# A transformer block with experts on one core: ring rooms given to the experts one by one, the first modulation sum moved into attention, router weights held stationary

## The chip, the core and the metric

The kernel runs on one core of a Trainium2 chip. Its engines are TensorE (PE), VectorE (DVE), ScalarE (ACT), GpSimd (POOL) and SyncE (SP), which here issues nearly all weight loads. The metric is the time of one execution on the device in microseconds, lower is better. The time before is 2291.39 us, the median of 3 runs (2287.88 to 2292.07).

## The reference, cut to what matters

512 tokens of width 1024, all in float32. A first block mixes tokens by attention and a gated linear recurrence, then sends tokens to 16 experts; a second block follows (convolution, pooling and a dense feed-forward part) that the change does not touch.

```python
mod = (silu(c) @ ada_w + ada_b)                      # ada_w is (1024, 6144)
shift1, scale1, gate1, shift2, scale2, gate2 = split(mod, 6)
h = rms_norm(x, norm_mix_w) * (1 + scale1) + shift1
# token_mixer: projections by w_in, attention o_att, recurrence o_hg, then
merged = sigmoid(g0) * (o_att @ w_branch_att) + sigmoid(g1) * (o_hg @ w_branch_hg)
x = x + gate1 * (merged @ w_out)
h = rms_norm(x, norm_ffn_w) * (1 + scale2) + shift2
# expert_choice_ffn
affinity = softmax(h @ w_router)                     # (512, 16)
top_w, top_idx = top_k(affinity.T, 64)               # each expert takes 64 tokens
hid = silu(h[top_idx] @ w_gate[e]) * (h[top_idx] @ w_up[e])    # 64 x 2048
x = x + gate2 * scatter_add(top_w * (hid @ w_down[e]))
```

## The kernel before

Everything is written engine by engine, with semaphores between engines; no scheduler moves anything. The order of work on an engine is the order of its code, partly woven from generators by `weave`, which takes one step of each in turn.

**The ring.** All weights arrive in pieces of 1 MB (128 partitions x 2048 floats) in rooms of SBUF called slots. There are 15: slots 0 to 5 are the ring proper, slots 6 to 14 lie in the work area and become free only when the token mixer's tensors there are dead. `ring_plan` writes down, for each piece, its slot; SP goes through that list in order (L385 to L402), waits for the last reader of the piece that was in the slot (`last_reader`), and issues the load. As SP works in order, a piece whose slot is not free holds back all behind it. An expert has 24 pieces, `eg` and `eu` (a gate and an up piece for each of 8 blocks k of the input width) and 8 of `ed` (down); 16 experts have 384. The first 15 go to rooms named by `cycle`; from then on a piece waits for the one 15 places ahead of it to be read.

**The modulation (ada).** `ada_w` comes as 24 pieces, 8 for each third of `mod`. `ada_step` on DVE (L1449) multiplies a piece by a column of silu(c) and adds it to an accumulator of 128 x 2048. Two sums over the partitions follow on PE: `ada_cols` (L423, L425) gives 8 columns by matmuls that move one column each, and a bias by one-row matmuls; `ada_row` (L698, L699) gives a row of 512 repeated on all partitions, by a matmul with a stationary block of ones and one with a one-row bias. Pieces 8 to 15 give gate1 and shift2, pieces 16 to 23 give scale2 and gate2.

**The merge loop**, `for d in range(8)` at L702: eight blocks of 128 output channels. For d of 4 and more PE first computes the two gate projections (`c0`, `c1`), then for all d the two branch projections (`cb`, first half into bank b0+2, second into b0+3). DVE multiplies and adds them (L1644, L1646, L1649, semaphores mg_a, mg_b, mg_m) and then takes ada steps: 1 after each of d = 0 to 3, 3 after each of d = 4 to 7. After d = 5 PE runs `ada_row` and `ada_cols` on the first sum, after d = 7 `ada_cols` and `ada_row` on the second.

**From w_out to the experts.** `out_proj` (L758) makes 8 units u of w_out, DVE adds each to x (L1673, L1675), and then x is normed, transposed by PE (`turn`, L437), scaled by DVE and ACT by turns into H2T, and `logits(k)` (L799) multiplies block k of H2T by 16 columns of the router's weights, two blocks behind the transposes. DVE takes the softmax and then finds 64 tokens for each of 16 experts by eight rounds of max and match_replace (L1701, L1702); L817 turns the mask, L822 counts positions. `gather` (L837) then picks the tokens, and the experts start (L879 gate and up, L915 down).

Attention and the second half of the recurrence run before the merge loop in one weave, on each engine:

```python
            weave(fill, lv, fill, att, fill, att, fill)
```

Here `lv` is a level of the recurrence (DVE: L1554 to L1572), `att` a step of attention (DVE: L1600 to L1607), `fill` the gate projections of PE (L622).

Of the kernel before, what the change touches and what calls it, by code (L numbers as in the profile page):

```python
# [10 lines left out]
ALU = mybir.AluOpType  # L11
# [58 lines left out]
MG, ACC2 = QQ, TTA  # L70
X = QT
# [29 lines left out]
def ring_plan():  # L101
# [7 lines left out]
    more = [("bg", h, br) for h in range(2) for br in range(2)]  # L109
    ada = 8  # L110
    for half in range(4):
        if half >= 2:
            more += [("c0", half), ("c1", half)]
        more.append(("cb", half))
        n = 2 if half < 2 else 6
        more += [("ada", ada + i) for i in range(n)]
        ada += n
    slots += [(4, 5, 0, 1, 2)[i % 5] for i in range(len(more))]
    keys += more + [("wo", n) for n in range(4)]
    slots += [3, 1, 2, 4]  # L120
# [5 lines left out]
    cycle = (11, 12, 13, 14, 5, 0, 3, 1, 2, 4, 7, 8, 9, 10, 6)  # L126
# [60 lines left out]
def build(nc, t, out):  # L187
    with ExitStack() as ctx:
# [194 lines left out]
        def _(e):  # L383
            for key, (slot, _, before) in plan.items():
# [21 lines left out]
        def _(e):  # L406
# [284 lines left out]
            def ada_row(half, dst_n):  # L691
                for i in range(2):
                    n, bk = half * 1024 + 512 * i, 2 + i

                    e.wait_ge(s["mg_a" if i == 0 else "mg_b"], 5 if half == 0 else 7)
                    if half == 1:
                        e.wait_ge(s["ar_a"], i + 1)
                    e.matmul(bank(bk), ones, at(ACC2 + n, 512), start=True, stop=False)  # L698
                    e.matmul(bank(bk), one_row, rows(0, 1, ADAB + n, 512), start=False, stop=True).then_inc(s["ar_pe"], 1)  # L699


            for d in range(8):  # L702
# [20 lines left out]
                if j == 0:  # L723
                    e.wait_ge(*got[kb])

# [6 lines left out]
                else:  # L732
                    e.wait_ge(s["mg_a"], d - 1)
                    if d == 6:
                        e.wait_ge(s["ar_a"], 1)
# [3 lines left out]
                elif d >= 2:  # L739
                    e.wait_ge(s["mg_b"], d - 1)  # L740
                    if d == 6:
                        e.wait_ge(s["ar_a"], 2)
                    if d == 7:
                        e.wait_ge(s["ad_d"], 1)
# [1248 lines left out]
```

## Time and profile before

| | |
|---|---|
| median of 3 runs | 2291.39 us |
| the profiled execution, its own time | 2292.04 us |
| its span in the profile | 2290.2 us |
| PE busy | 2031.2 us (89%), 8478 instructions |
| DVE busy | 606.4 us (26%) |
| ACT busy | 412.6 us (18%) |
| DMA | 513.37 MB, 224 GB/s over the span |
| the chain that ended last | PE 71%, DMA 18%, DVE 5%, ACT 4% |

A float32 matmul is two records of a MATMUL and of a weight load each, so counts in the rows below are twice those of the code. The clock column PEclk gives the granted TensorE clock as a share: 1.00 is the level of 2.4 GHz, 0.50 that of 1.2 GHz. A stretch in the windows view lists busy time and instructions of PE, PE's weight loads, DVE, ACT and POOL, then PEclk, the share of DMA and GB/s. In the order rows further down, which show the program and no time, a matmul is one row.

### The profile page before, as it was taken

Reading aid. Unit: us, or ns where it says so; the run is one execution under the profiler, and the core shown is the slowest. Engines: PE = TensorE matmul, PEld = TensorE weight load, DVE = VectorE, ACT = ScalarE, POOL = GpSimd, SP = SyncE. Lnnn points to the kernel's source line nnn. Section 1 sums busy time; section 2 is a strip of 40 time slices with the busy share of each in tenths; the row PEclk is TensorE's granted clock in tenths of the full one; section 3 lists DMA queues with packets and bytes.
Section 4 is the critical chain, followed back from the end, with each engine's and each line's share of the span. In section 5 each row is a group of like instructions: output and inputs, shape, how many; then the busy total and the mean of one; then the engine's idle time right before and its main releaser. Section 6 shows DMA issues by size and latency. Waiting matters only on the chain.

```text
span 2290.2 us, 19692 instructions
## 1 busy us (share of the span) xinstructions
PE 2031.2 (89%) x8478; PEld 1145.7 (50%) x8478; DVE 606.4 (26%) x867; ACT 412.6 (18%) x621; POOL 32.8 (1%) x42
## 2 busy tenths in 40 slices
PE   3986999999897998888888889888879998999997
PEld 2543465544486343434343434233334487888785
DVE  4152335332323001010101111100127714222233
ACT  2123545510011000000000000000020213222222
POOL 0000000000000000000000000000030000000000
PEclk9998999997795999999999999999989998999998
DMA  8210111134632999999999999999962123322210
GB/s 327 74 37 19 37 37 56 37 111 165 249 130 91 416 416 416 416 416 416 416 416 416 416 416 416 416 416 417 417 219 74 37 68 93 97 92 93 91 37 37
DMA packets 143787, 513.37 MB, mean 224 GB/s; under 512 B 7891, under 2 KB 70355, under 8 KB 107731
## 3 DMA queue, kind: packets, MB, share of 16 engines
q1 hardware_dynamic: 141632, 503.35, 56.2%
q10 hardware_dynamic: 2070, 8.78, 0.9%
q8 instruction: 67, 1.10, 0.2%
q14 instruction: 18, 0.15, 0.0%
HBM read 510.00 MB, written 2.10 MB: 224 GB/s over the span
## 4 chain that ended last, share of the span: by engine, by line
PE 71%; DMA 18%; DVE 5%; ACT 4%; issue 1%; SPq 1%; POOL 0%; ACTq 0%; DVEq 0%; POOLq 0%
PE ps L412 14%; DMA work<-in_w_exp_up 11%; PE ps L915 11%; PE ps L879 6%; PE ps L417 6%; DMA ring<-in_w_exp_up 6%; PE ps L1058 5%; PE ps L1017 4%; PE ps L1019 4%; PE ps L1018 4%; PE ps L837 3%; PE ps L622 2%; DMA ring<-in_ada_w 2%; PE ps L567 1%; PE ps L860 1%
## 5 line engine op out<-in xcount | busy, mean ns | idle before, releaser
L879 PE MATMUL ps<-work 128*64 128x512 f32 x1232 | 312.9, 595 | 43.2 <-DMA work<-in_w_exp_up 43.2
L412 PE MATMUL ps<-work,ring 128*128 128x512 f32 x784 | 344.6, 598 | 0.8 <-DVE work L1588 0.8
L412 PEld LDWEIGHTS ps<-work,ring 128*128 128x128 f32 x784 | 149.0, 192 | 187.8 <-issue 186.1
L879 PE MATMUL ps<-ring,work 128*64 128x512 f32 x816 | 217.4, 595 | 24.3 <-DMA ring<-in_w_exp_up 24.3
L879 PEld LDWEIGHTS ps<-work 128*64 128x64 f32 x1232 | 107.3, 137 | 220.7 <-issue 138.8
L1750 DVE TENSOR_TENSOR work<-work,ps 64x512 f32<-64x512 f32 x64 | 42.0, 691 | 507.9 <-ACT work L1320 507.3
L1320 ACT ACTIVATE work<-ps 64x512 f32<-64x512 f32 x64 | 32.6, 584 | 758.4 <-PE ps L879 758.4
L915 PE MATMUL ps<-work 128*64 128x512 f32 x600 | 143.1, 634 | 5.2 <-issue 4.7
L879 PEld LDWEIGHTS ps<-ring,work 128*64 128x64 f32 x816 | 74.6, 137 | 140.6 <-issue 92.5
L417 PE MATMUL ps<-ring,work 128*128 128x256 f32 x640 | 142.8, 386 | 0.9 <-ACT work L1350 0.9
L1017 PE MATMUL ps<-xh,wh 128*128 128x512 f32 x352 | 137.8, 391 | 1.0 <-issue 1.0
L1018 PE MATMUL ps<-xl,wh 128*128 128x512 f32 x352 | 137.6, 391 | 0.0
L1019 PE MATMUL ps<-xh,wl 128*128 128x512 f32 x352 | 137.4, 390 | 0.0
L417 PEld LDWEIGHTS ps<-ring,work 128*128 128x128 f32 x640 | 123.8, 194 | 22.4 <-issue 5.2
L1854 DVE TENSOR_TENSOR wl<-ring,wh 128x2048 fp32r<-128x2048 f32 x32 | 73.4, 2292 | 186.3 <-ACT wh L1389 186.3
L915 PE MATMUL ps<-ring,work 128*64 128x512 f32 x424 | 100.3, 628 | 3.1 <-issue 3.1
L1058 PE MATMUL ps<-wh,xh 128*128 128x512 f32 x352 | 96.4, 396 | 5.6 <-issue 5.6
L915 PEld LDWEIGHTS ps<-work 128*64 128x64 f32 x600 | 53.0, 145 | 86.8 <-issue 86.8
L1762 DVE TENSOR_TENSOR work<-ps,stay 64x512 f32<-64x512 f32 x32 | 22.0, 688 | 276.1 <-PE ps L915 275.6
L1389 ACT ACTIVATE wh<-ring 128x2048 fp32r<-128x2048 f32 x33 | 63.1, 1913 | 176.1 <-PE ps L1019 93.9
L1058 PEld LDWEIGHTS ps<-wh,xh 128*128 128x128 f32 x352 | 67.3, 192 | 20.1 <-issue 6.0
L860 PE MATMUL ps<-work 128*128 128x512 f32 x128 | 66.4, 630 | 9.7 <-DVE work L1741 8.1
(229 smaller groups left out, 1928.5 us busy)
## 6 DMA issues: line engine op xcount, KB each, us to landing
work<-in_w_exp_gate SPq DMA_DIRECT2D x77, 1024.0 KB, 23.0
work<-in_w_exp_up SPq DMA_DIRECT2D x77, 1024.0 KB, 23.2
work<-in_w_exp_down SPq DMA_DIRECT2D x75, 1024.0 KB, 21.0
ring<-in_w_exp_down SPq DMA_DIRECT2D x53, 1024.0 KB, 20.9
ring<-in_w_exp_gate SPq DMA_DIRECT2D x51, 1024.0 KB, 22.7
ring<-in_w_exp_up SPq DMA_DIRECT2D x51, 1024.0 KB, 23.2
ring<-in_w_in SPq DMA_DIRECT2D x27, 1024.0 KB, 6.9
ring<-in_ada_w SPq DMA_DIRECT2D x24, 1024.0 KB, 5.6
```

The lines of the kernel that those rows point to most:

```text
L412: i = e.matmul(bank(bk), piece(key)[:, off + k, 128 * j:128 * j + 128], rhs(k), start=(k == 0), stop=(k == nk - 1))
L417: i = e.matmul(bank(bk, n, o), lhs(k, tc), piece(key)[:, k, c0:c0 + n], start=(k == 0), stop=(k == 7))
L837: i = e.matmul(bank(5 + k // 4, 128, 128 * (k % 4)), at(XS2 + 1024 * c + 128 * k, 128), at(OH + 128 * c, 128), start=(c == 0), stop=(c == 3))
L860: e.matmul(bank(6 + dh), at(OHWT + 128 * tc, 128), at(YE + 512 * dh, 512), start=True, stop=True).then_inc(s["x_cb"], 1)
L879: i = e.matmul(PS[64 * gu:64 * gu + 64, fb, :], at(XET + 128 * k + 64 * z, 64), flat(key)[:, 512 * fb:512 * fb + 512], start=(k == 0), sto ...
L915: i = e.matmul(PS[64 * dh:64 * dh + 64, 4, :], at(HIDT + 64 * (2 * n + k), 64), piece(key, 2)[:, k, 512 * dh:512 * dh + 512], start=(n + k ...
L1017: e.matmul(bank(bk), WH[i][:, o:o + 128], XH[:, x], start=(k == 0), stop=False)
L1018: e.matmul(bank(bk), WH[i][:, o:o + 128], XL[:, x], start=False, stop=False)
L1019: p = e.matmul(bank(bk), WL[i][:, o:o + 128], XH[:, x], start=False, stop=(k == KD - 1))
L1058: p = e.matmul(bank(2 * tc + dh), l[:, o], w[i][:, 1024 * k + 512 * dh:1024 * k + 512 * dh + 512], start=(f == 0 and q == 0), stop=(f == F ...
L1389: e.activation(WH[i][:, :], flat(("ff", f)), ACT.Copy).then_inc(s["fs_h"], 1)
L1854: e.tensor_tensor(WL[i][:, :], flat(("ff", f)), WH[i][:, :].bitcast(F32), ALU.subtract).then_inc(s["fs_l"], 1)
```

## The change

1. **Rooms one by one.** The order in which the first 15 expert pieces take rooms is new, and each room of the work area has a wait of its own instead of one for nearly all of them. Most of them are now asked for before or early in w_out.
2. **First modulation sum during attention.** Pieces 8 to 15 go into an accumulator of their own, ACC1, in the room of GATE1 and GATE2, one step for each round of the weave. Their two sums on PE move from behind d = 5 into d = 6. The second sum's steps follow 1, 1, 1, 1, 2, 2 times after d = 0 to 5 and no longer after d = 6 and 7; its sums on PE stand behind units 1 and 2 of w_out. DVE's scale2 comes after unit 1.
3. **Stationary router weights.** `logits(k)` is one matmul that holds 16 columns of the router stationary and moves 512 tokens, in place of four that hold 128 tokens and move 16 columns. The logits then lie with experts on partitions; a copy by DVE and four transposes (`by_token`) bring them back. The counting of positions takes 4 matmuls of 64, 48, 32 and 16 columns in place of 10 of 16.
4. x is loaded before the merge loop in place of after it, and DVE's scratch in w_out moves from PT to YE.

```diff
+ACC1 = GATE1
-    slots += [(4, 5, 0, 1, 2)[i % 5] for i in range(len(more))]
-    slots += [3, 1, 2, 4]
+    bg = [("bg", h, br) for h in range(2) for br in range(2)]
+    ada = lambda i: [(("ada", 8 + 2 * i), 4), (("ada", 9 + 2 * i), 5)]
+    more = [(bg[0], 0)] + ada(0) + [(bg[1], 1), (bg[2], 2)] + ada(1) + [(bg[3], 0)] + ada(2)
+    rest = [("cb", 0), ("cb", 1), ("c0", 2), ("c1", 2), ("cb", 2), ("c0", 3), ("c1", 3), ("cb", 3)]
+    for i, key in enumerate(rest):
+        more += [(key, (1, 2, 0)[i % 3])] + (ada(3 + i) if i < 5 else [])
+    more += [(("wo", n), (3, 4, 5, 0)[n]) for n in range(4)]
-    cycle = (11, 12, 13, 14, 5, 0, 3, 1, 2, 4, 7, 8, 9, 10, 6)
+    cycle = (8, 11, 12, 13, 14, 10, 9, 1, 2, 7, 3, 4, 5, 0, 6)
...
-                if key[0] in ("eg", "eu") and before is None and slot >= 11:
-                    e.wait_ge(s["mg_pb"], 8)
-                if key[0] in ("eg", "eu") and before is None and 6 <= slot <= 10:
-                    e.wait_ge(s["wo_pe"], 8)
-                    e.wait_ge(s["wo_x"], 8)
-                    e.wait_ge(s["ar_pe"], 4)
-                    if slot == 6:
+                if key[0] in ("eg", "eu") and before is None:
+                    if slot == 8:
+                        e.wait_ge(s["mg_m"], 1)
+                    elif slot >= 11:
+                        e.wait_ge(s["mg_pb"], 8)
+                    elif slot >= 9:
+                        e.wait_ge(s["mg_m"], 8)
+                    elif slot == 7:
+                        e.wait_ge(s["ac_pe"], 3)
+                        e.wait_ge(s["ar_pe"], 4)
+                    elif slot == 6:
+                        e.wait_ge(s["wo_pe"], 8)
                         e.wait_ge(s["rt_pe"], 1)
...
+                if d == 6:
+                    e.wait_ge(s["d_ada"], 16)
+                    e.wait_ge(s["l_ab"], 32)
+                    e.wait_ge(s["mg_a"], 6)
+                    ada_row(ACC1, 0, 6)
+                    e.wait_ge(s["mg_b"], 6)
+                    ada_row(ACC1, 512, 7)
...
+                if d == 6:
+                    e.wait_ge(s["ar_a"], 1)
+                    ada_cols(ACC1, 1, 6, 0, True).then_inc(s["ac_pe"], 1)
+
+            def second_gate(u):
+                if u == 1:
+                    e.wait_ge(s["d_ada"], 24)
+                    e.wait_ge(s["l_ab"], 48)
+                    e.wait_ge(s["mg_b"], 8)
+                    ada_cols(ACC2, 0, 7, 0, True).then_inc(s["ac_pe"], 1)
+                    e.wait_ge(s["mg_a"], 8)
+                    ada_row(ACC2, 1024, 6)
+                elif u == 2:
+                    e.wait_ge(s["ad_d"], 2)
+                    ada_row(ACC2, 1536, 7)
...
-                for tc in range(TC):
...
-                    p = e.matmul(bank(4 + tc, 16), at(H2T + 512 * k + 128 * tc, 128), at(O_VEC + VEC["wr"][0] + 16 * k, 16),
-                                 start=(k == 0), stop=(k == KD - 1))
+                return e.matmul(PS[0:16, 4, :], at(O_VEC + VEC["wr"][0] + 16 * k, 16), at(H2T + 512 * k, 512), start=(k == 0), stop=(k == KD - 1))
...
-            for tc in range(TC):
-                for c in range(tc + 1):
-                    p = e.matmul(bank(4, 16, 16 * tc), tri if c == tc else ones, at(mskT + 16 * c, 16), start=(c == 0), stop=(c == tc))
+            for back in range(TC):
+                p = e.matmul(bank(4, 64 - 16 * back, 16 * back), tri if back == 0 else ones, at(mskT, 64 - 16 * back), start=(back == 0), stop=(back == 3))
...
+            def ada_first():
+                for i in range(8, 16):
+                    ada_step(i, ACC1)
+                    yield
-            weave(fill, lv, fill, att, fill, att, fill)
+            weave(fill, lv, fill, att, fill, att, fill, ada_first())
...
-                for _ in range(1 if d < 4 else 3):
+                for _ in range(1 if d < 4 else 2 if d < 6 else 0):
...
+            e.wait_ge(*rooted(2, 3))
+            e.tensor_copy(rows(0, 16, WKT, 512), PS[0:16, 4, :]).then_inc(s["rt_d"], 1)
```

On PE, from the merge loop's last blocks to w_out, before (L412 is a dense block of the merge loop, 8 rows to a projection of eight blocks k; L698, L699 are `ada_row`, L423, L425 `ada_cols`, L417 w_out):

```order
L412 MATMUL ps<-work,ring 128x512 x80
L698 MATMUL ps<-work,stay 128x512
L699 MATMUL ps<-work,stay 128x512
L423 MATMUL ps<-stay,work 128x1
L425 MATMUL ps<-stay,work 128x1
...
L412 MATMUL ps<-work,ring 128x512 x48
L423 MATMUL ps<-stay,work 128x1
L425 MATMUL ps<-stay,work 128x1
...
L698 MATMUL ps<-work,stay 128x512
L699 MATMUL ps<-work,stay 128x512
L417 MATMUL ps<-ring,work 128x256 x128
```

The same place of the change, where these lines are L416, L696, L697, L427, L429 and L421:

```order
L416 MATMUL ps<-work,ring 128x512 x96
L696 MATMUL ps<-stay 128x512
L697 MATMUL ps<-work,stay 128x512
...
L416 MATMUL ps<-work,ring 128x512 x8
L427 MATMUL ps<-stay 128x1
L429 MATMUL ps<-stay,work 128x1
...
L416 MATMUL ps<-work,ring 128x512 x24
L421 MATMUL ps<-ring,work 128x256 x32
...
L421 MATMUL ps<-ring,work 128x256 x16
...
L421 MATMUL ps<-ring,work 128x256 x80
```

The first `ada_row` now has 16 more dense matmuls ahead of it, 8 dense ones stand between it and `ada_cols`, and d = 7 runs straight into w_out, whose units 0 and 1 (x32) and 2 (x16) come ahead of the second sum's parts.

On DVE, one round of the attention weave: before, the last share of attention (L1607) is followed at once by the next level of the recurrence (L1554).

```order
L1600 TENSOR_REDUCE stay<-ps 128x1
L1601 TENSOR_SCALAR stay<-stay 128x1
L1606 RECIPROCAL stay<-stay 128x1
L1607 TENSOR_SCALAR work<-work,stay 128x512
L1554 TENSOR_TENSOR work<-work 128x2x128x4
```

In the change (L1616 is the share, L1563 the level) an ada step stands between them, once in each of eight rounds.

```order
L1609 TENSOR_REDUCE stay<-ps 128x1
L1610 TENSOR_SCALAR stay<-stay 128x1
L1615 RECIPROCAL stay<-stay 128x1
L1616 TENSOR_SCALAR work<-work,stay 128x512
L1465 SCALAR_TENSOR_TENSOR stay<-ring,stay 128x2048
L1563 TENSOR_TENSOR work<-work 128x2x128x4
```

On PE, the router before: transposes (L437), four logits matmuls a block (L799), then the turns of the affinities and of the mask, and the ten of the count.

```order
L437 MATMUL ps<-stay,work 128x128 x4
L799 MATMUL ps<-stay,work 128x16 x12
L813 MATMUL ps<-stay 16x128 x4
L817 MATMUL ps<-stay,work 128x16 x4
L822 MATMUL ps<-stay 128x16 x10
L837 MATMUL ps<-work 128x128 x32
```

And in the change: one matmul a block (L804), one more set of turns (the first L816), and four for the count (L831).

```order
L441 MATMUL ps<-stay,work 128x128 x4
L804 MATMUL ps<-work,stay 16x512 x3
L816 MATMUL ps<-stay,work 128x16 x4
L824 MATMUL ps<-stay 16x128 x4
L816 MATMUL ps<-stay,work 128x16 x4
L831 MATMUL ps<-stay 128x64
L831 MATMUL ps<-stay 128x48
L831 MATMUL ps<-stay 128x32
L831 MATMUL ps<-stay 128x16
L846 MATMUL ps<-work 128x128 x32
```

## Rows read from the trace of the kernel before

**Rows 1.** Windows: the last router stretch, the first experts, the other experts.

```profile
709.00:741.30 32.30, 18.44 (x106) 15.81 (x108) 14.36 (x33) 2.79 (x5) 0.00 (x0) 0.63 0.02 9
741.30:841.00 99.70, 95.30 (x486) 41.79 (x482) 10.52 (x18) 9.03 (x21) 0.00 (x0) 0.98 1.01 409
841.00:1683.00 842.00, 742.79 (x3422) 306.98 (x3418) 109.95 (x176) 60.95 (x143) 0.00 (x0) 0.98 1.01 413
```

**Rows 2.** Timeline of SP's issues, 607 to 745 us: start, us, what.

```profile
612.78 0.43 SPq L402 DMA_DIRECT2D ring<-in_w_exp_up  x1
...
705.61 0.33 SPq L402 DMA_DIRECT2D work<-in_w_exp_gate  x1
...
741.34 0.33 SPq L402 DMA_DIRECT2D work<-in_w_exp_up  x1
```

**Rows 3.** The chain that ended last, 532 to 681 us: start, us, what.

```profile
532.70 0.70 DVE work L1646
...
534.18 2.27 DVE work L1456
...
552.79 44.47 PE ps L412 x96
...
597.64 6.99 DMA ring<-in_ada_w
...
604.72 2.36 DVE work L1456
...
623.42 57.33 PE ps L417 x256
```

**Rows 4.** Windows: ada_row, ada_cols, then dense work at the higher clock.

```profile
536.00:544.50 8.50, 8.00 (x8) 2.00 (x8) 0.44 (x1) 0.60 (x1) 0.00 (x0) 0.50 1.04 378
544.50:552.70 8.20, 8.20 (x33) 7.96 (x32) 0.00 (x0) 0.60 (x1) 0.00 (x0) 0.50 0.51 162
560.00:565.00 5.00, 5.00 (x13) 2.20 (x12) 0.00 (x0) 0.60 (x1) 0.00 (x0) 1.00 0.18 77
630.00:680.00 50.00, 50.00 (x234) 44.01 (x233) 11.43 (x18) 4.06 (x7) 0.00 (x0) 1.00 0.30 112
```

**Rows 5.** The chain near the start: ada_cols, transposes, dense matmuls, all at clock 1.00.

```profile
35.51 6.99 PE ps L423 x32
42.49 5.76 PE ps L437 x32
48.26 41.20 PE ps L412 x96
```

**Rows 6.** Timeline of DVE: a round of the attention weave, and an ada step.

```profile
375.03 0.49 DVE L1607 TENSOR_SCALAR work<-work,stay 128x512 f32<-128x512 f32 x1
378.53 1.23 DVE L1554 TENSOR_TENSOR work<-work 128x1024 f32<-128x1024 f32 x1 [3.01 <-PE ps L567]
...
479.16 2.35 DVE L1456 SCALAR_TENSOR_TENSOR work<-ring,stay,work 128x2048 f32<-128x2048 f32 x1
```

**Rows 7.** The chain in the logits: one block's transposes, then its matmuls.

```profile
689.81 0.93 PE ps L437 x4
690.74 1.52 PE ps L799 x8
```

**Rows 8.** Windows: the logits as a whole.

```profile
690.00:705.00 15.00, 15.00 (x75) 15.00 (x73) 1.62 (x2) 3.61 (x4) 0.00 (x0) 0.50 0.37 153
```

**Rows 9.** The chain in the routing: a copy of 16x512, mask turns, position count.

```profile
708.15 0.69 DVE work L1698
...
721.27 0.62 PE ps L817 x4
...
722.19 4.46 PE ps L822 x20
```

**Rows 10.** Windows: transposes alone ahead of the second block, then what follows.

```profile
1702.50:1705.50 3.00, 3.00 (x16) 3.00 (x15) 1.13 (x2) 1.37 (x2) 3.00 (x6) 0.50 0.00 0
1706.00:1709.00 3.00, 3.00 (x14) 1.77 (x13) 0.96 (x3) 1.33 (x2) 3.00 (x6) 1.00 0.02 5
```

More of the change, by code:

```diff
@@ L108, in ring_plan @@
     slots = [i % 6 for i in range(len(keys))]
[L109 to L117, printed above, removed]
-    slots += [(4, 5, 0, 1, 2)[i % 5] for i in range(len(more))]
-    keys += more + [("wo", n) for n in range(4)]
-    slots += [3, 1, 2, 4]
+    bg = [("bg", h, br) for h in range(2) for br in range(2)]
[5 more added lines that the diff above has]
+    more += [(("wo", n), (3, 4, 5, 0)[n]) for n in range(4)]
+    keys += [key for key, _ in more]
+    slots += [slot for _, slot in more]
     ex = []
@@ L689, in _, with ada_row @@
             weave(fill, lv, fill, att, fill, att, fill)
[L691 to L699, printed above, removed]
+            def ada_row(acc, n, bk):
+                e.matmul(bank(bk), ones, at(acc + n, 512), start=True, stop=False)
+                e.matmul(bank(bk), one_row, rows(0, 1, ADAB + n, 512), start=False, stop=True).then_inc(s["ar_pe"], 1)
             for d in range(8):
@@ L769, in out_proj @@
                         p.then_inc(done, 1)
+                        behind(4 * h + n)
             def wo_free(u):
@@ L1649, in _ @@
                 e.tensor_tensor(at(MG + 512 * d, 512), at(s0, 512), at(s1, 512), ALU.add).then_inc(s["mg_m"], 1)
-                for _ in range(1 if d < 4 else 3):
-                    if ada == 16:
-                        e.wait_ge(s["ac_pe"], 2)
-                        e.tensor_copy(at(sh2, 8), bank(7, 8)).then_inc(s["ad_d"], 1)
+                for _ in range(1 if d < 4 else 2 if d < 6 else 0):
                     ada_step(ada, ACC2)
                     ada += 1
-            e.wait_ge(s["ac_pe"], 3)
-            e.scalar_tensor_tensor(out=at(sc2, 8), in0=bank(7, 8), scalar=1.0, in1=vec("nfw"),
-                                   op0=ALU.add, op1=ALU.mult).then_inc(s["ad_d"], 1)
+                if d == 6:
+                    e.wait_ge(s["ac_pe"], 2)
+                    e.tensor_copy(at(sh2, 8), bank(6, 8)).then_inc(s["ad_d"], 1)
             e.wait_ge(s["l_x"], 32)
@@ L1675, in _ @@
                     e.tensor_tensor(xa, xa, ta, ALU.add).then_inc(s["wo_x"], 1)
+                    if u == 1:
+                        e.wait_ge(s["ac_pe"], 3)
+                        e.scalar_tensor_tensor(out=at(sc2, 8), in0=bank(7, 8), scalar=1.0, in1=vec("nfw"),
+                                               op0=ALU.add, op1=ALU.mult).then_inc(s["ad_d"], 1)
                 def r2_ready(c):
@@ L1695, in _ @@
             e.tensor_tensor(r3(aff), r3(lg), r16(rst + 8), ALU.mult).then_inc(s["rt_d"], 1)
-            e.wait_ge(s["rt_pe"], 2)
-            e.wait_ge(*rooted(2, 3))
-            own(e.tensor_copy(rows(0, 16, AFFT, 512), PS[0:16, 5, :]))
+            e.wait_ge(s["rt_pe"], 3)
+            own(e.tensor_copy(rows(0, 16, AFFT, 512), PS[0:16, 4, :]))
             for r in range(CAP // 8):
```

84 lines of the change are left out of this document (35 added, 49 removed).

## Prediction

> **What bounds the kernel now.** I read the windows by stage first, then SP's issues, then the chain of waits. From 741.3 to 1683 us DMA is busy all the time and moves 409 to 413 GB/s [rows 1]: the experts are bound by their weights. When that stretch begins is decided on PE. SP issues the last of the first 15 expert pieces at 705.61, has no free room left, and issues the 16th only at 741.34, when PE has read the first piece [rows 2]; in between DMA is idle (9 GB/s from 709 to 741.3, [rows 1]). From there the remaining 369 pieces of 1 MB follow at a fixed rate (1683 - 741.3 = 942 us, 2.55 us a piece), and behind them comes a second block that nothing here touches. So a microsecond gained ahead of 741 is gained at the end, one for one, and the date at which the first 15 pieces land is worth nothing as long as they are there. The sum is therefore one about the chain from the merge loop to the first gather.
>
> In that chain [rows 3] two waits stand out. PE has finished d = 5 at 532.67; then come DVE's L1646 (0.70), L1649 (as long) and an ada step (2.27), and `ada_row` starts at 536.50, a stall of 3.8 us. After d = 7, at 597.3, PE waits for an ada piece (DMA, to 604.63) and its step (2.36), 9.9 us. The windows add a third cost: after each stall the granted clock is 0.50, through `ada_row` and `ada_cols`, and back at 1.00 only some us into dense work [rows 4].
>
> **Rooms one by one: nothing.** The edit moves issues of expert pieces earlier, into idle DMA time. What hides it is the wait for room number 16, above. The last room, slot 6, is still tied to `rt_pe` 1, and 15 pieces are read in the old order of positions afterwards. x comes earlier too; it delayed only DVE. Both 0.
>
> **Ada steps in attention: nothing, under a thin cover.** A step is 2.35 us of DVE. In each round DVE is idle for 3.01 us at just the place where it goes, between L1607 and L1554 [rows 6]; that round stands for eight, the others read 3.0 to 3.9 or more, and the first step is a short one. So it ends about 0.6 us before the level's matmul that DVE waits for. The pieces: two rooms (4, 5) go round between eight steps 12 us apart, and a piece needs 7 us (6.99, [rows 3]). Without that cover, each round would pay up to 2.4 us, 19 us in all.
>
> **The chain from 532.67 to 680.75.** It takes 148.1 us now. Prices at clock 1.00: a dense record of 512 columns 0.43 (41.20 / 96, [rows 5]), one of w_out 0.214 (50 / 234, [rows 4]); `ada_cols`, 32 records, 7.0 at 1.00 [rows 5] and 8.2 at 0.50 [rows 4]; `ada_row`, 8 records for two rows, 8.1 at 0.50 (from 536.5 to 544.6, [rows 4]). At 1.00 no row shows it: at least 8 x 0.43 = 3.4, at most the 8.1; I take 4.1, half and nearest the dense record, as the same columns move. What a restart of the clock costs: 44.47 - 96 x 0.43 = 3.2 in d = 6 and 7, 57.33 - 256 x 0.214 = 2.6 in w_out [rows 3].
>
> New: the gate projections of d = 6, 32 x 0.43 = 13.8; `ada_row` behind them without a stall (its own steps are over since attention, and DVE's work after d = 5, the merge and two steps, is 6.2 us beside 13.8 us of PE), at 1.00, 4.1; the branch projections 6.9; `ada_cols` 7.6 (it starts at 1.00 and ends, I assume, at 0.50); d = 7 20.6 + 2.9 for the restart; then a new wait, since w_out's unit 0 stands straight behind d = 7 and needs the merged block: L1646 and L1649, 1.5; units 0 and 1, 13.7; `ada_cols` 7.6; first half of the second `ada_row` at 0.50, 4.0; unit 2, 6.9 + 2.6; second half at 1.00, 2.1; units 3 to 7, 34.2. The sum is 128.5, **19.6 less**. Queued behind the wait on DVE for `ac_pe` 3 (after unit 1) are only the sums of units 2 and later, which PE reaches 14 us later.
>
> **Routing.** The copy of 16x512 (0.69) and the turns back (0.62) are new on the path, 1.4 with their hand-overs. The count has 8 records in place of 20: 4.46 x 12/20 = 2.7 less [rows 9]. Together **1.3 less**.
>
> **Logits.** Now a block takes 4 transposes (0.93) and 8 records (1.52), 2.45, so 19.6 for eight [rows 7], all at clock 0.50 [rows 8]. New: 0.93 and 2 records that move 512 columns. At 0.50 such a record costs between 0.86 (twice 0.43) and 1.01 (8.1 / 8 in `ada_row`); at 0.95 a block is 2.83, eight are 22.6, **3.0 more**. The question is whether the clock stays. The old loop moves 16 columns at a time and kept 0.50 for 15 us of unbroken work [rows 8]. The new loop is made of transposes and 512-column matmuls. Transposes alone are shown to bring the clock back: in 1702.5 to 1705.5 PE does 16 of them and nothing else at 0.50, and then stands at 1.00 [rows 10]. For dense matmuls of 512 and 256 columns it came back too [rows 4]. It did not come back in `ada_row`, half of whose matmuls have one row. So I expect it back some 5.5 us into the loop, as the restarts above cost 2.6 to 3.2 us, half of their length. Then at 1.00 a block costs 4 x 0.18 (5.76 / 32, [rows 5]) + 0.86 = 1.6: 5.5 + 9.2 = 14.7, **4.9 less**.
>
> A page speaks against this step. The Trainium skill, "TensorE: Matmul & The Clock Gate", Part 4, says that a transpose does not count as busy time for the clock gate. This case's trace does not agree ([rows 10], 0.50, then 1.00 with transposes alone before). By the page's rule the transposes would not help and the clock would likely stay at 0.50, so that the sum would be 3.0 more and not 4.9 less, case (a) below.
>
> **Sum.** 19.6 + 1.3 + 4.9 = 25.8 from the profiled execution's own 2292.04 gives 2266.2; the median before is 0.65 lower, so 2265.6. I say 2266.
>
> **The rivals.**
> (a) The clock stays at 0.50 in the logits, since a matmul with 16 stationary columns may not act as a full one: 19.6 + 1.3 - 3.0 = 17.9 less, 2273.5. For it: no row here has 16 stationary columns and many moved ones.
> (b) The clock does not fall in `ada_cols` when it enters at 1.00. The only `ada_cols` at 1.00 is [rows 5], and the clock stayed there, but PE had had nothing to do in the 35 us ahead of it, and it had stayed through that as well. Then the restarts (2.9 + 2.6), twice 0.6 of `ada_cols` and 2 of the half row fall away: 7 to 9 more, 2258.
> (c) The cover in attention is too thin, or DVE is late for w_out: part is given back. A third of the saving lost is 8 us; with half a dozen rounds late by 2 us, 12. 2276 to 2288. The cover of 3.01 against 2.35 speaks against it.
> (d) The change does not do what it says for the total: the expert stream is not released by PE but ends at its own date, so that PE only waits longer at the experts. Then 2291, no change. The idle DMA from 709 to 741.3 [rows 1] speaks against it.
> (e) Slower: DVE works in order, so when an ada step's piece has not landed in a round, attention and the recurrence both stand. Two rooms serve the eight steps, and SP takes the branch gates' pieces in the same list ahead of some of them, so that a piece can hang on a room that PE frees a round later. It decides from 25.8 / 8 = 3.2 us a round beyond the gap on; a full round late (12 us) in three rounds would be 36 less 26, 2301. By the list the pieces are asked for 20 us or more ahead of their step, which speaks against it.
>
> **How the numbers follow.** The main case (back in the logits, down in `ada_cols`) has 0.48, and by itself runs from 2262 to 2270 (ada_row between 3.4 and 8.1, restarts between 2.6 and 3.2, record between 0.86 and 1.01). (a) 0.23, (b) 0.14, (c) 0.09, (d) 0.03, (e) 0.03. The range of 8 in 10 takes the main case, (a) whole and most of (b): 2257 to 2277. A measurement of this kernel can tell 0.2%, 4.6 us, from no change. Faster by more: the first three and all of (c), 0.94; within it (d), 0.03; slower (e), 0.03.
>
> **What the profile of the changed kernel would show.** PE without a gap from d = 0 to the end of d = 7, then 1.5 us idle before w_out. Clock 1.00 in the first `ada_row`, and four records of it per 2 us. The 16th expert piece issued at about 715 to 717, the DMA then at 410 GB/s for 942 us as before. In attention, DVE's ada steps between L1616 and L1563 with some 0.6 us of idle left, and PE with no new wait there. In the logits blocks of 2.8 us first and of 1.6 us later, or of 2.8 throughout in case (a). The prediction is wrong if the stretch from the 16th piece to the end of the experts is not 942 us, if PE waits in attention, or if the clock drops in places where PE is now meant to run through.

## The result and the profile after

The changed kernel takes 2252.91 us (median of 4 runs, 2251.59 to 2256.67), the kernel before beside it 2291.14 us: a ratio of 0.9838, 95% interval 0.9821 to 0.9855. That is 38.2 us less, where I had forecast 25 and a range that ended at 2257. Two repeats of the unedited change, told below, gave 2254.30 and 2258.05 us; the median of all 12 runs of it is 2255.3. The profiled execution took 2251.97 us with a span of 2250.2, 40.0 less than the span before.

The chain that ended last, from the merge loop to the end of w_out, in the changed kernel (start, us, what):

```profile
466.55 79.23 PE ps L416 x184
545.79 0.86 PE ps L696 x2
546.65 1.05 PE ps L697 x2
...
549.80 7.06 PE ps L416 x16
...
556.98 0.31 PE ps L429 x2
...
561.63 22.51 PE ps L416 x48
...
584.16 0.70 DVE work L1661
...
585.79 14.05 PE ps L421 x64
...
602.79 0.52 PE ps L427 x2
...
605.87 2.01 PE ps L696 x2
...
609.88 8.57 PE ps L421 x32
618.45 0.86 PE ps L696 x2
...
620.35 34.74 PE ps L421 x160
```

Against [rows 3] both stalls are gone: dense work runs unbroken from 466.55 to 545.79, through the place where PE used to stop at 532.67, and between d = 7 and w_out only the merge (1.6 us) is left. The first `ada_row` takes 4.0 us for its two rows (0.86 to 1.05 a pair of records) in place of 8.1.

The same chain through the router:

```profile
660.46 2.10 PE ps L441 x9
662.55 1.70 PE ps L804 x2
664.25 0.59 PE ps L441 x4
664.85 0.96 PE ps L804 x2
...
671.05 2.69 PE ps L804 x6
...
673.76 0.69 DVE work L1706
...
674.50 0.43 PE ps L816 x4
...
691.20 1.90 PE ps L831 x8
...
694.36 9.20 PE ps L846 x64
703.56 27.67 PE ps L888 x128
```

The first logits matmul still runs at the lower clock (1.70 us a pair), all later ones at the higher (0.96, then 0.90), and four transposes fall from 0.93 to 0.59 [rows 7]. The windows say the same (columns as in [rows 1]):

```profile
549.80:556.80 7.00, 7.00 (x19) 3.17 (x18) 0.69 (x1) 0.60 (x1) 0.00 (x0) 1.00 0.00 0
556.87:561.60 4.73, 4.73 (x33) 4.49 (x32) 1.38 (x2) 0.00 (x0) 0.00 (x0) 1.00 0.01 3
561.63:564.00 2.37, 2.37 (x3) 1.09 (x4) 0.17 (x1) 0.00 (x0) 0.00 (x0) 0.50 0.01 3
...
664.30:673.70 9.40, 9.40 (x34) 2.93 (x34) 1.62 (x2) 3.61 (x4) 0.00 (x0) 1.00 0.01 2
```

`ada_cols` (556.87 to 561.6) begins at 1.00, the clock falls at its end, and d = 7 starts at 0.50. In the router the clock is back at 1.00.

SP's issues of the 15th and 16th expert pieces, which answer to [rows 2]:

```profile
673.82 0.33 SPq L406 DMA_DIRECT2D work<-in_w_exp_gate  x1
707.17 0.33 SPq L406 DMA_DIRECT2D work<-in_w_exp_up  x1
```

The 16th goes out at 707.17 in place of 741.34, 34.2 us earlier. From the merge loop's start to the first gate and up matmul it is now 237.0 us (466.55 to 703.56), before 270.6 (467.16 to 737.73). I use that distance below, as it leaves out what shifts the start of the loop from one execution to the next (465.7 to 468.0).

| stretch | before | after | less | forecast |
|---|---|---|---|---|
| up to the merge loop | 467.2 | 466.6 | 0.6 | 0 |
| merge loop and w_out | 213.6 | 188.6 | 25.0 | 19.6 |
| norm (to the first transposes) | 5.4 | 5.4 | 0 | 0 |
| logits | 19.4 | 13.3 | 6.1 | 4.9 |
| softmax, choice, count | 22.4 | 20.6 | 1.8 | 1.3 |
| first gather | 9.8 | 9.2 | 0.6 | 0 |
| first gate matmul to the end | 1552.5 | 1546.6 | 5.9 | 0 |

So two things have to be explained: 7.7 us more than forecast ahead of the experts, and 5.9 from the first gate matmul on, where nothing was changed.

### The profile page after: what moved, and what is told of

It is laid out like the page before. It is cut to its first block, busy times and chain, and to the rows that moved or that the text cites. A ratio compares the mean times of both kernels' runs of the same rounds, so it can differ in the third digit from the quotient of the medians.

```text
span 2250.2 us, 19571 instructions
## 1 busy us (share of the span) xinstructions
PE 2005.9 (89%) x8422; PEld 1117.0 (50%) x8422; DVE 606.8 (27%) x868; ACT 412.6 (18%) x621; POOL 32.7 (1%) x42
## 4 chain that ended last, share of the span: by engine, by line
PE 71%; DMA 18%; DVE 5%; ACT 4%; issue 1%; SPq 0%; POOL 0%; ACTq 0%; DVEq 0%; POOLq 0%
PE ps L416 15%; DMA work<-in_w_exp_up 13%; PE ps L924 11%; PE ps L888 7%; PE ps L421 6%; PE ps L1067 5%; DMA ring<-in_w_exp_up 4%; PE ps L1026 4%; PE ps L1028 4%; PE ps L1027 4%; PE ps L846 3%; PE ps L626 3%; PE ps L571 1%; DMA ring<-in_ada_w 1%; PE ps L869 1%
## 5 line engine op out<-in xcount | busy, mean ns | idle before, releaser
L888 PE MATMUL ps<-work 128*64 128x512 f32 x1256 | 351.6, 595 | 40.3 <-DMA work<-in_w_exp_up 40.3
L416 PE MATMUL ps<-work,ring 128*128 128x512 f32 x784 | 344.6, 598 | 0.8 <-DVE work L1597 0.8
L888 PE MATMUL ps<-ring,work 128*64 128x512 f32 x792 | 242.6, 595 | 23.7 <-DMA ring<-in_w_exp_up 23.7
L416 PEld LDWEIGHTS ps<-work,ring 128*128 128x128 f32 x784 | 149.0, 192 | 187.9 <-issue 186.3
L888 PEld LDWEIGHTS ps<-work 128*64 128x64 f32 x1256 | 116.0, 137 | 230.3 <-issue 154.0
L888 PEld LDWEIGHTS ps<-ring,work 128*64 128x64 f32 x792 | 80.5, 137 | 128.1 <-issue 82.3
L421 PE MATMUL ps<-ring,work 128*128 128x256 f32 x640 | 141.3, 383 | 2.5 <-DVE work L1664 1.7
L924 PE MATMUL ps<-work 128*64 128x512 f32 x600 | 140.0, 618 | 3.7 <-issue 3.1
L421 PEld LDWEIGHTS ps<-ring,work 128*128 128x128 f32 x640 | 122.2, 192 | 24.9 <-issue 8.4
L924 PE MATMUL ps<-ring,work 128*64 128x512 f32 x424 | 108.0, 658 | 4.7 <-issue 4.7
L924 PEld LDWEIGHTS ps<-work 128*64 128x64 f32 x600 | 52.2, 143 | 84.5 <-issue 84.5
## 6 DMA issues: line engine op xcount, KB each, us to landing
ring<-in_w_exp_up SPq DMA_DIRECT2D x51, 1024.0 KB, 22.4
```

The costliest lines, as they stand in the source:

```text
L416: i = e.matmul(bank(bk), piece(key)[:, off + k, 128 * j:128 * j + 128], rhs(k), start=(k == 0), stop=(k == nk - 1))
L421: i = e.matmul(bank(bk, n, o), lhs(k, tc), piece(key)[:, k, c0:c0 + n], start=(k == 0), stop=(k == 7))
L888: i = e.matmul(PS[64 * gu:64 * gu + 64, fb, :], at(XET + 128 * k + 64 * z, 64), flat(key)[:, 512 * fb:512 * fb + 512], start=(k == 0), sto ...
L924: i = e.matmul(PS[64 * dh:64 * dh + 64, 4, :], at(HIDT + 64 * (2 * n + k), 64), piece(key, 2)[:, k, 512 * dh:512 * dh + 512], start=(n + k ...
```

## The experiments

In the runs named e1 to e12 the kernel before took 2291.6 to 2292.7 us beside them, in the last four 2291.47.

**e1, the router alone.** The kernel before with part 3 of the change and nothing else:

```diff
-                    p = e.matmul(bank(4 + tc, 16), at(H2T + 512 * k + 128 * tc, 128), at(O_VEC + VEC["wr"][0] + 16 * k, 16),
-                                 start=(k == 0), stop=(k == KD - 1))
+                return e.matmul(PS[0:16, 4, :], at(O_VEC + VEC["wr"][0] + 16 * k, 16), at(H2T + 512 * k, 512), start=(k == 0), stop=(k == KD - 1))
...
+            by_token()
...
+            for back in range(TC):
+                p = e.matmul(bank(4, 64 - 16 * back, 16 * back), tri if back == 0 else ones, at(mskT, 64 - 16 * back), start=(back == 0), stop=(back == 3))
```

> The kernel before with the third part alone (stationary router weights, logits turned back, four matmuls for the count). My theory: the first gather comes 7.5 to 8.5 us earlier (logits 13.3 us in place of 19.4, from the copy to the count 20.6 in place of 22.4) and the total follows one for one: 2283 us. Rival: the parts lean on each other, because the clock enters the logits in another state in the old surroundings; then the clock stays at 0.50 and the total is 2291 to 2294.

It took 2283.64 us against 2292.70, ratio 0.9959 (0.9947 to 0.9972), 9.1 us less; the distance was 263.7 us (466.59 to 730.26), 6.9 less than before and a little under the 7.5 I gave. The part works by itself. What is missing lies in the logits: they took 14.4 us, as the clock came back 6.4 us into them (first group of four transposes at 0.59 us at 691.93, first transpose at 685.50), where in the change it came back after 3.8 us and they took 13.3.

**e2, the router undone.** The changed kernel with the old router.

```diff
-                return e.matmul(PS[0:16, 4, :], at(O_VEC + VEC["wr"][0] + 16 * k, 16), at(H2T + 512 * k, 512), start=(k == 0), stop=(k == KD - 1))
+                for tc in range(TC):
...
+                    p = e.matmul(bank(4 + tc, 16), at(H2T + 512 * k + 128 * tc, 128), at(O_VEC + VEC["wr"][0] + 16 * k, 16),
+                                 start=(k == 0), stop=(k == KD - 1))
```

> The changed kernel with the old router. My theory: rooms and modulation sums are worth 25 us of chain and 2 to 6 us of clock in later stages, so 2260 to 2263 us. Rival (the parts do not add up): the two parts alone sum to clearly less or more than the 38 us of both.

2265.04 us, ratio 0.9877 (0.9863 to 0.9890); distance 244.4 us (467.82 to 712.21), 26.2 less. 26.2 and 6.9 are 33.1, both together gave 33.6: the parts add up. The total was 2 us above what I expected, since that had the 2 to 6 us of later stages in it.

**e3, late rooms.** The changed kernel with the waits for rooms of before:

```diff
-                    if slot == 8:
-                        e.wait_ge(s["mg_m"], 1)
...
+                if key[0] in ("eg", "eu") and before is None and 6 <= slot <= 10:
+                    e.wait_ge(s["wo_pe"], 8)
+                    e.wait_ge(s["wo_x"], 8)
+                    e.wait_ge(s["ar_pe"], 4)
-    cycle = (8, 11, 12, 13, 14, 10, 9, 1, 2, 7, 3, 4, 5, 0, 6)
+    cycle = (11, 12, 13, 14, 1, 2, 3, 4, 5, 0, 7, 8, 9, 10, 6)
```

> The changed kernel with the old waits for the rooms of the work area, so that only 4 expert pieces are asked for before the first w_out units end and 10 come after unit 6 or later. My theory: all 15 are in SBUF before the first gather ends, the 16th is asked for at the same time, and the total stays within 1 us of 2253. Rival (the rooms matter): the experts' first pieces are late, or DMA runs behind from the start, and the total rises by the amount of weights not loaded by then, up to 10 pieces or 25 us.

The distance was 237.1 us (468.04 to 705.14) against 237.0: the early rooms are worth nothing, as they only fill time in which DMA would otherwise load later and still in time. The total was 2258.64 us (2253.89 to 2259.24). That is not within 1 us of 2253, and at first it looked like a cost of 5 us; the last four runs below show that it is the other length of the last stretch, here 1552.1 us.

**e4, the second sums ahead of w_out.**

```diff
+            second_gate(1)
+            second_gate(2)
-            out_proj("wo", lambda k, tc: at(MG + 512 * k + 128 * tc, 128), s["wo_pe"], wo_free, lambda: e.wait_ge(s["mg_m"], 8), second_gate)
+            out_proj("wo", lambda k, tc: at(MG + 512 * k + 128 * tc, 128), s["wo_pe"], wo_free, lambda: e.wait_ge(s["mg_m"], 8))
```

> The changed kernel with the second modulation sum's parts on PE behind d = 7 and ahead of w_out, as in the kernel before, the steps on DVE staying early. My theory: the ada wait of 9.9 us and the stall of 3.8 are gone because the steps are early; the place behind units 1 and 2 is worth the hidden merge wait or less: here the merge (1.6 us) is hidden by ada_cols, but both rows of ada_row run at clock 0.50 (2 us more), so within 2 us of the change. Rival: the place is what counts, since PE has to wait there for DVE or for the bias row: 5 us or more slower.

2260.88 us (2260.39 to 2262.45), distance 239.7 us (466.88 to 706.62), 2.7 more than the change. Its chain:

```profile
589.91 0.52 PE ps L427 x2
...
594.94 2.00 PE ps L696 x2
596.95 2.00 PE ps L697 x2
598.95 57.44 PE ps L421 x256
```

Both rows of `ada_row` run at 2.0 us a pair and w_out starts at the lower clock, 57.44 as in [rows 3]. It is a little more than the 2 us I gave, far from the rival's 5. So of the 25 us by far the most do not hang on the second sum's new place. That they come from the early steps on DVE fits the two stalls that are gone, but no run put the steps back alone, and e4 kept the first sum inside d = 6, so that share is argued and not measured.

**e5 and e11, more DVE work in attention.** One more pass over the sum behind each ada step (e5), then two, as here:

```diff
+                    for _ in range(2):
+                        own(e.tensor_scalar(at(ACC1, 2048), at(ACC1, 2048), 1.0, None, ALU.mult))
```

> The changed kernel with a second pass of DVE over the accumulator (128x2048, multiplied by one) behind each of the eight ada steps in attention. My theory: 0.8 us of idle time is left in each round, a pass costs 1.3 to 2.4 us, so each round grows by 0.5 to 1.6 us where DVE's level is on the path, 4 to 13 us in all, 2257 to 2266. Rival (attention does not hang on DVE there, the cover is wider than the gap): within 1 us of 2253.

> The changed kernel with two more passes of DVE over the accumulator behind each ada step in attention. One pass cost PE nothing: it ate the 0.8 us before the level and half of the 1.0 us before the next share. A second pass of 1.25 us finds about 0.4 us of reserve, so by the trace each of the eight rounds grows by 0.5 to 0.9 us on PE, 4 to 7 us in all, and the merge loop starts at 470 to 473 us. Rival (attention has more reserve, in the buffers of shares and scores): it starts at 466 to 467 as before.

Neither cost PE anything. The merge loop started at 465.76 and 466.98, the distances were 237.0 and 237.1 us; the totals 2255.43 and 2258.05 lie within the scatter of the change (2251.6 to 2259.3). DVE's timeline in the changed kernel and then in e11:

```profile
374.94 2.35 DVE L1465 SCALAR_TENSOR_TENSOR stay<-ring,stay 128x2048 f32<-128x2048 f32 x1
378.09 1.23 DVE L1563 TENSOR_TENSOR work<-work 128x1024 f32<-128x1024 f32 x1 [0.81 <-PE ps L571]
```

```profile
375.26 2.35 DVE L1465 SCALAR_TENSOR_TENSOR stay<-ring,stay 128x2048 f32<-128x2048 f32 x1
377.64 2.49 DVE L1638 TENSOR_SCALAR stay<-stay 128x2048 f32<-128x2048 f32 x2
380.16 1.23 DVE L1563 TENSOR_TENSOR work<-work 128x1024 f32<-128x1024 f32 x1
```

In e11 the level comes 2.5 us after the step in place of 0.8, and DVE is never idle there. Still PE's waits from 340 us to the merge loop (line, what it waits for, us in all, times, longest) are in both the same three:

```profile
PE ps L609 <- DVE work L1593: 3.5, 1, 3.5
PE ps L615 <- ACT work L1214: 1.6, 2, 0.8
PE ps L416 <- DVE work L1597: 0.8, 1, 0.8
```

The kernel before has them too, with the same times. Both my expectations were wrong: the idle gap before an instruction is not the whole of its reserve. In e11 DVE's level ends at 384.2 us, and PE's next level matmuls start at 388.3.

**e6, the old logits behind all transposes,** in the kernel before.

```diff
-            turn(XS2, [0, 1, 2, 3], lambda c: normed(2, c), t2_free, s["t_pe"], lambda k: logits(k - 2) if k >= 2 else None)
-            logits(KD - 2)
+            turn(XS2, [0, 1, 2, 3], lambda c: normed(2, c), t2_free, s["t_pe"])
+            for k in range(KD - 1):
+                logits(k)
```

> The kernel before, with the eight blocks of logits behind all transposes in place of between them. Theory from the trace (transposes bring the clock back): within 3 to 7 us of unbroken transposes the clock stands at 1.00, and the last transposes take 0.59 us for four in place of 0.93. Rival (the Trainium skill, TensorE: Matmul & The Clock Gate, Part 4, transposes do not count): 0.50 throughout, 0.93 for four to the end. The time of the whole: 2289 to 2292 by the first, 2291 to 2293 by the second.

2288.51 us (10 runs) against 2291.88, ratio 0.9983 (0.9973 to 0.9992), distance 267.5 us (465.74 to 733.25), 3.1 less. The windows: transposes, their end, then the matmuls that move 16 columns.

```profile
684.60:688.00 3.40, 3.35 (x16) 3.35 (x17) 1.62 (x2) 1.05 (x2) 0.00 (x0) 0.50 0.97 386
688.00:690.80 2.80, 2.80 (x17) 2.80 (x15) 1.32 (x2) 1.28 (x2) 0.00 (x0) 0.56 1.01 427
690.90:694.00 3.10, 3.10 (x29) 3.10 (x29) 0.20 (x1) 2.05 (x2) 0.00 (x0) 0.98 1.00 412
694.00:698.00 4.00, 4.00 (x20) 4.00 (x20) 0.00 (x0) 0.00 (x0) 0.00 (x0) 0.50 0.08 33
```

With nothing but transposes behind it on PE the clock rises from 0.50 to 1.00 by 690.9; and then, with PE busy all the time on 16-column matmuls, it is at 0.50 again from 694. For the rule of the Trainium skill, "TensorE: Matmul & The Clock Gate", Part 4, that a transpose does not count for the clock gate, this trace is the counterexample, with the float32 transposes of this kernel. The old loop was held at the lower clock by its logits, not by its transposes.

**e7, the new logits behind all transposes.** The same edit in the changed kernel.

> The changed kernel with its eight logits matmuls behind all transposes. If transposes alone bring the clock back, it stands at 1.00 before the first logits matmul, and 16 stationary columns keep it there: 16 records of 0.43 to 0.48 us. From the first transpose to the copy 12.5 to 13 us in place of 13.3; total within 1 us of the change in the same state. Rival: matmuls with 16 stationary columns alone let the clock fall, so that the later ones take 0.86 us or more, and the stretch takes 15 us.

```profile
661.05 5.05 PE ps L441 x29
666.10 6.99 PE ps L804 x16
```

16 records at 0.437 us, the clock at 1.00 throughout: matmuls with 16 stationary columns and 512 moved ones held the clock. To the copy it takes 12.0 us in place of 13.3. The distance was 236.4 (467.12 to 703.54), only 0.6 less, since the first gather then took 9.8 us in place of 9.2. The total, 2257.72, is that of the longer last stretch (1552.6).

**e8, the first `ada_cols` behind d = 7**, to fill the wait for the merge.

```diff
-                if d == 6:
-                    e.wait_ge(s["ar_a"], 1)
-                    ada_cols(ACC1, 1, 6, 0, True).then_inc(s["ac_pe"], 1)
+                if d == 7:
+                    e.wait_ge(s["mg_a"], 7)
+                    ada_cols(ACC1, 1, 2, 0, True).then_inc(s["ac_pe"], 1)
```

> The changed kernel with the first ada_cols moved from behind d = 6 to behind d = 7, where PE waits 1.6 us for the last merge. Theory: the wait is filled, the rest is equal, 1.5 us less at the first gather. Rival: the clock falls there and w_out's first units run at 0.50, or w_out's unit 2 waits for the copy of shift2; then nothing or 1 us more. In the total either is at the limit of what can be told.

Distance 236.5 us (466.40 to 702.94), 0.5 less; 2255.40 us. The wait of 1.6 is gone. The clock now falls just before w_out, as the rival said, and its first 64 records take 15.63 us in place of 14.05; but the second `ada_cols` then takes 4.8 in place of 6.0, and the router's first transpose starts 192.3 us after the merge loop's start in place of 193.9, 1.6 less, as the theory said. Behind it the logits took 0.7 more and the first gather 0.4 more, by the clock's restarts. So neither side was simply right, and half a microsecond in the distance tells nothing of a place in the code.

**e12, e7 and e8 together.**

> The changed kernel with the first ada_cols behind d = 7 and the logits behind all transposes, to see if the two add up to something that can be told. By the runs so far 0.5 us from the first and 0.6 us from the second: first gate and up matmul at 702.3, the total not to be told from the change. Rival: the clock's state at w_out and at the logits shifts, 1 to 2 us worse.

2254.92 us, ratio to the kernel before 0.9844 (0.9829 to 0.9859), distance 233.1 us (467.10 to 700.15), 4.0 less than the change where I expected about 1. Up to the router e12 is e8, and still its first transpose came after 190.6 us and not 192.3: unit 2 of w_out took 8.51 us here and 10.16 there. So the same code differed by 1.6 us in the distance by one restart of the clock. In time e12 cannot be told from the change; its profile had the longer last stretch again.

**e9, `ada_cols` without bias matmuls** (shift2 lacks its bias), a single run.

```diff
-                    ada_cols(ACC1, 1, 6, 0, True).then_inc(s["ac_pe"], 1)
+                    ada_cols(ACC1, 1, 6, 0, False).then_inc(s["ac_pe"], 1)
```

> The changed kernel without the bias matmuls of the first ada_cols: 16 records in place of 32, so shift2 lacks its bias. It measures the price that I got wrong. Theory: a record with a stationary block of 128 rows costs 0.218 us at clock 1.00, as near the start, and one with a single row nearly nothing (2 x 0.155 - 0.218 = 0.09): 16 records take 3.5 us. Rival: every record costs 0.155 in this place and the ones near the start were slowed by something else: 2.5 us.

```profile
558.26 1.68 PE ps L427 x16
```

1.68 us, 0.105 a record: neither theory. With bias the block took 4.76 (556.87 to 561.63), so the 16 records of one-row matmuls added 3.1, nearly twice what those of the 128-row ones cost. Whether the one-row matmuls themselves cost it, or the change from one form to the other at each column, no run tells apart. And 0.105 is just half of the 0.218 of [rows 5], the row from which I had priced `ada_cols` at clock 1.00.

The trace of the kernel before explains that row. Its own list of the granted clock begins only at 46.90 us, with 1.00, and where it has no entry the windows view shows 1.00. The 32 transposes behind that `ada_cols` run through this moment:

```profile
43.00:46.00 3.00, 3.00 (x16) 3.00 (x15) 1.61 (x2) 0.78 (x1) 0.00 (x0) 1.00 1.09 349
47.00:48.00 1.00, 1.00 (x12) 1.00 (x11) 0.85 (x2) 0.58 (x1) 0.00 (x0) 1.00 1.09 348
```

16 in 3.0 us is the pace of transposes at 0.50 in [rows 10], 12 in 1.0 us is far above it. So PE ran at 0.50 up to 46.9 us, by the doubled price of its records in `ada_cols` too, and the 1.00 that I read there was no reading at all.

**e10, e13 to e16: the last stretch.** e10 and e13 are the change unedited, e14 is the change and e15 and e16 are the kernel before, with the experts started a little later by copies on DVE ahead of the first gather, two in e14 and e15, four in e16 as here:

```diff
+            for _ in range(4):
+                own(e.tensor_copy(rows(0, 16, AFFT, 512), rows(0, 16, WKT, 512)))
```

> The changed kernel once more, with nothing edited, for its scatter. In the first profile of it the stretch from the first gate and up matmuls to the end took 1546.6 us; in the kernel before and in the four variants so far it took 1551.5 to 1552.5. Theory: the clock's restarts fell luckily in that one execution, by 5 us, and a second profile shows about 1552 and a time near 2256; the runs scatter between 2251 and 2257. Rival: the change itself shortens the later stages by 5 us, and the second profile shows 1547 again.

> The changed kernel a third time, nothing edited. Theory (the start decides, with some jitter): times in two groups, near 2252 and near 2256, and the stretch from the first gate and up matmul to the end either 1547 or 1552 us, as the time says. Rival (a property of the change): 1547 again whatever the time.

> The changed kernel with two more copies of 16x512 on DVE (1.4 us) ahead of the first gather. Theory (the start decides): fewer or none of the runs in the short group, the stretch 1552 in the profile, the total 1.4 us up by the delay and up to 5 more, 2254 to 2259. Rival (a property of the change): the stretch stays 1547, the total is 1.4 us up.

> The kernel before with the same 1.4 us. By the theory that the start decides, its stretch may become 1547 in some runs, which gives a total 4 us below 2293; with no luck it stays 1552 and the total is 2293. Rival: 1552 always, total 2293.

> The kernel before with 2.9 us more ahead of the first gather. As the run with 1.4 us: by the theory one of the two has runs with a stretch of 1547 and totals 4 to 6 us under 2294.5; by the rival both have 1552 always and this one is at 2294.5.

| run | median us (runs) | first gate matmul at | distance from the merge loop | from first gate matmul to the end |
|---|---|---|---|---|
| before | 2291.14 (4) | 737.7 | 270.6 | 1552.5 |
| change | 2252.91 (4) | 703.6 | 237.0 | 1546.6 |
| e10, change again | 2254.30 (4) | 703.5 | 237.0 | 1546.6 |
| e13, change again | 2258.05 (4) | 704.6 | 237.1 | 1552.0 |
| e14, change, two copies | 2257.83 (4) | 704.0 | 237.5 | 1551.4 |
| e15, before, two copies | 2292.20 (11) | 738.2 | 271.1 | 1552.0 |
| e16, before, four copies | 2287.49 (11) | 739.4 | 271.5 | 1546.3 |
| e1 to e9, e11, e12 | | | | 1551.5 to 1552.6 |

The copies did not delay by the 1.4 and 2.9 us of my expectations. One takes 0.43 us on the chain, as here in e16, and not the 0.7 I had assumed, so they add 0.9 and 1.8 us:

```profile
727.88 0.43 DVE work L1744
```

And the first gather gives half of it back: it took 9.81 us in the kernel before, 9.34 in e15 and 8.93 in e16. In all three it begins at 0.50, and the clock is back at 1.00 between 732.9 and 733.7 us, whether it began at 727.9, 728.8 or 730.4. So the experts started only 0.5 and 1.0 us later, counted from the merge loop.

e10 came out as its rival said, 1546.6 again, but e13, with nothing edited either, took 1552.0: that decides against a property of the change. e14 and e15 had no run in the short group. e16 does more work than the kernel before and is 4 us faster in the median; its runs fall in two groups, five from 2285.1 to 2286.7, one at 2287.5 and five from 2290.7 to 2293.7, so that the ratio to the kernel before is only 0.9991 (0.9981 to 1.0000). The kernel before seems to reach the short stretch by itself too, if seldom: of its 54 runs two lie near 2288 (2287.88, 2287.64), all others above 2290. So the shorter stretch is no property of the change. Three places of the chain in e16 that make it up (last down projection, w_out_2, last down part), and the same in e13:

```profile
1667.76 13.95 PE ps L915 x64
...
1826.88 55.51 PE ps L417 x256
...
2147.23 117.07 PE ps L1058 x509
```

```profile
1633.62 16.04 PE ps L924 x64
...
1795.32 56.97 PE ps L421 x256
...
2116.79 118.36 PE ps L1067 x509
```

2.1, 1.5 and 1.3 us; the second block's 29 transposes give 0.5 more. In the longer case each of these begins at granted clock 0.50 or falls to it. In the shorter one the first two run at 1.00 from their start, and the last begins at 0.50 too but is back at 1.00 earlier. In the kernel before, w_out_2 begins at 0.50, in the change at 1.00, behind the same short wait:

```profile
1829.00:1832.00 3.00, 3.00 (x8) 2.37 (x9) 0.00 (x0) 0.00 (x0) 0.00 (x0) 0.50 0.04 11
```

```profile
1791.00:1795.00 4.00, 3.64 (x17) 3.25 (x18) 0.00 (x0) 0.22 (x1) 0.00 (x0) 1.00 0.11 37
```

All of them go together, in each of the 18 profiles. What exactly an execution must hit was not found: by the trace's zero the change at 703.5 hit it twice, e7 at 703.5 and e8 at 702.9 did not. Counted from the first entry of the granted clock (at 45.3 to 47.9 us in these traces) they do sort: the last down projection begins at 1586.06 and 1586.05 us in the two short profiles of the change, and at 1585.6 (e7), 1585.9 (e8), 1586.2 (e5) and 1586.4 to 1586.5 (e3, e11, e13, e14) in long ones, the rest farther off. That a few tenths of a microsecond against the clock's own timing decide is what this suggests; no run tests it.

## Why the prediction was right or wrong

**What bounds the kernel: right.** 34.2 us earlier at the 16th piece, and the experts' stream unchanged: to the last up piece it is 916 us from there in both (741.34 to 1657.7, 707.17 to 1623.8). e1 and e2 show gains ahead of it passed on, though not quite "one for one": the gather's clock restart gave back half of the delays of e15 and e16. The sign that I had named, 942 us from the 16th piece to the end of the experts, failed: it was 941.6 before and 939.0 in the change, by the last down projection (16.57 and 13.95), which belongs to the last paragraph below.

**Rooms worth nothing: right** (e3, 237.1 against 237.0). That the earlier x is worth nothing was not tested.

**Ada steps under a thin cover: right in the price, wrong in "thin".** They cost nothing; 0.8 us of idle was left where I had said 0.6, but the cover reaches at least 2.5 us a round further (e11). Rival (c) had no ground.

**The chain to the end of w_out: right in mechanism, 5.4 us mis-sized.** The term that failed is "`ada_cols` 7.6", twice: they took 4.8 and 6.0, 4.4 less in all. I had taken 7.0 at clock 1.00 from [rows 5], a row that ran at 0.50 (see e9) and has no bias matmuls in it. The same misreading was the ground of rival (b), that PE's 35 idle us there had left the clock at 1.00, and of the 0.18 us for a transpose at 1.00, which takes 0.15. The restarts, forecast at 2.9 and 2.6, took 1.9 (22.51 for 48 records) and 1.7 (8.57 for 32). `ada_row` at 1.00, 4.1 forecast, took 4.0; the merge wait 1.5 took 1.6; the clock fell in `ada_cols` as assumed, so rival (b) did not come about, and that the time is below its 2258 comes from other terms. The rest, units 0 and 1 and 3 to 7, came out 0.9 higher than forecast.

**Logits: right,** 6.1 in place of 4.9. The clock was back 3.8 us into the loop, not 5.5. The same part in the old surroundings (e1) had it back after 6.4 us, so the 1.2 us beyond my forecast are luck: they hang on when the router happens to begin, which no row had shown me. Rival (a) is excluded by this and by e7, and so is the rule of the Trainium skill, "TensorE: Matmul & The Clock Gate", Part 4, on which it leaned, by [rows 10] and by e6, where nothing but transposes ran before the clock rose.

**Count and turns: right in kind,** 1.8 in place of 1.3. The copy took 0.69 and the turns 0.43; the count 1.90 for 8 records, where by proportion it was 1.8. Not in my sum: the turns of the affinities now run at 1.00 and take 0.62 in place of 1.04, and the first gather takes 0.6 less, as its clock is back sooner after its start.

**The end: the step that failed altogether is "behind them comes a second block that nothing here touches".** It is not touched, and still it and the last down projection ahead of it took 5.9 us less in that profile. That stretch has two lengths some 5.5 us apart, by what the granted clock is behind a few short waits, and one and the same program shows both. The sum had this term at nothing without a reason: I had one profile and took its last stretch for fixed. Of the 12 runs of the change five were near 2252 and the rest between 2253.9 and 2259.3. With the longer stretch alone the change would be at some 2257 us, at the edge of my range. Why one execution takes the one length and the next the other stays open.

## What to carry to other kernels

When weights stream at the full rate of DMA and a ring is full at their start, as here, ask only what lets the first room go again; loading the full ring earlier gained nothing. Take an engine's price from a row in the same state and form: a block priced from a row near the start of the trace, without its bias matmuls, was wrong by a third. Check a clock column against the pace of instructions whose price is known, above all near the start. Where stages behind a change begin after short waits, two executions of one program can differ by 0.2%; repeat the unedited kernel, or shift it on purpose as in e16, before such a difference is put down to an edit, and measure the shift in the trace.

## What was not expected of the hardware

- Under matmuls that move 16 columns the clock fell with PE busy all the time (e6, 1.00 to 0.50 at 694 us), while under those with 16 stationary columns and 512 moved ones it held (e7, 6.99 us at 1.00).
- One-row bias matmuls of one column, one behind each 128-row one, added 3.1 us for 16 records, where the 128-row ones alone took 1.68 (change against e9).
- The kernel before with 1.8 us of work added took 2287.49 us in place of 2291.47 in the median, with five of its eleven runs below 2287 (e16).
- A delay ahead of a stage that begins at clock 0.50 was half absorbed: 1.8 us more work in e16, and a gather of 8.93 in place of 9.81 us.
- The granted clock has no entry in the trace of the kernel before 46.90 us and reads 1.00 there, while PE's pace is that of 0.50.
